# Experts of a mixture in column tiles: four experts at a time, 96 rows each, weights through a ring of seven slots

## What is computed

```python
N_GROUPS, EXPERTS_PER_GROUP, TOP_K, D_MODEL, D_FF_EXPERT = 4, 8, 2, 1024, 512   # 32 experts
pg = softmax(x @ wrg + brg);  g_val, g_idx = top_k(pg, 1)          # one group per token
le = (x @ wre + bre)[group g_idx];  e_val, e_idx = top_k(le, 2)    # two experts of that group
e_w = softmax(e_val) * g_val;  expert = g_idx * 8 + e_idx
for every token and each of its two experts e:
    y[token] += e_w * ((silu(x @ wg[e]) * (x @ wu[e])) @ wd[e])
return h + y
```

## Time and profile before

| | us |
|---|---|
| median of 3 runs | 2239.81 |
| lowest and highest | 2235.87, 2240.45 |
| span of the profiled execution | 2236.3 |
| PE busy | 1933.4 (86%) |
| DVE, ACT, POOL busy | 584.9, 479.2, 104.5 |
| PE in the three products of the experts | 229.1 + 225.0 + 225.1 |

### The profile page before, as it was taken

The page is one execution under the profiler, slowest core; times in us unless marked ns, Lnnn a source line. Parts: engine busy times, 40 slices in busy tenths (PEclk is TensorE's granted clock), DMA queues, the critical chain, the costliest instruction groups (busy, mean ns, idle before and its releaser), DMA issues. The chain is left out here.

```text
span 2236.3 us, 18672 instructions
## 1 busy us (share of the span) xinstructions
PE 1933.4 (86%) x6294; PEld 1013.3 (45%) x6294; DVE 584.9 (26%) x1144; ACT 479.2 (21%) x1059; POOL 104.5 (5%) x143
## 2 busy tenths in 40 slices
PE   7899896888875789899599999379999999999990
PEld 3354743555542345555344544244444444444440
DVE  2111203676651233223222222411111111111114
ACT  2162101333322333333200000001111111111110
POOL 0000001000030000000000000000000000000003
PEclk9999997999996899989699999679999999999995
DMA  3310004111137100100151221357888888888847
GB/s 124 118 35 28 30 18 171 44 46 38 38 113 235 59 38 24 47 23 24 64 220 72 103 113 47 135 225 293 356 318 349 324 338 334 326 348 319 355 193 263
DMA packets 87624, 354.84 MB, mean 159 GB/s; under 512 B 14424, under 2 KB 38016, under 8 KB 74000
## 3 DMA queue, kind: packets, MB, share of 16 engines
q1 hardware_dynamic: 65488, 282.86, 33.1%
q0 software_dynamic: 12032, 43.52, 5.6%
q10 hardware_dynamic: 10064, 27.94, 3.2%
HBM read 292.81 MB, written 54.41 MB: 155 GB/s over the span
## 5 line engine op out<-in xcount | busy, mean ns | idle before, releaser
L1968 PE MATMUL ps<-eg,xsT 128*128 128x512 f32 x512 | 229.1, 601 | 4.5 <-DVE hid L1930 3.2
L1995 PE MATMUL ps<-ed,hT 128*128 128x512 f32 x512 | 225.1, 592 | 1.8 <-ACT hT L1899 1.8
L1981 PE MATMUL ps<-eu,xsT 128*128 128x512 f32 x512 | 225.0, 592 | 0.0
L1271 PE MATMUL ps<-wg,xt 128*128 128x512 f32 x432 | 207.8, 637 | 13.3 <-DMA xt<-xn_dram 8.8
L1941 DVE TENSOR_TENSOR xsT<-ps,wnT 128x512 f32<-128x512 f32 x64 | 41.2, 686 | 590.8 <-PE ps L1955 590.8
L243 PE MATMUL ps<-wbuf,wide 128*128 128x512 f32 (+3 forms) x464 | 171.4, 529 | 9.3 <-issue 9.3
L1968 PEld LDWEIGHTS ps<-eg,xsT 128*128 128x128 f32 x512 | 98.6, 193 | 129.2 <-issue 127.4
L1995 PEld LDWEIGHTS ps<-ed,hT 128*128 128x128 f32 x512 | 94.9, 190 | 109.7 <-issue 107.6
L1981 PEld LDWEIGHTS ps<-eu,xsT 128*128 128x128 f32 x512 | 94.9, 190 | 107.6 <-issue 107.6
L1271 PEld LDWEIGHTS ps<-wg,xt 128*128 128x128 f32 x432 | 85.9, 205 | 125.9 <-issue 110.2
L238 PE MATMUL ps<-wide,wbuf 128*128 128x512 f32 (+1 forms) x384 | 131.0, 505 | 11.2 <-issue 11.2
(11 more groups left out here) (321 smaller groups left out, 1908.5 us busy)
## 6 DMA issues: line engine op xcount, KB each, us to landing
eg<-w_expert_gate SPq DMA_DIRECT2D x32, 2048.0 KB, 13.2
eu<-w_expert_up SPq DMA_DIRECT2D x32, 2048.0 KB, 17.7
ed<-w_expert_down SPq DMA_DIRECT2D x32, 2048.0 KB, 8.4
y_dram<-ys ACTq DMA_DIRECT2D x32, 512.0 KB, 10.7
gt<-g_dram SPq DMA_DIRECT2D x9, 1024.0 KB, 5.8
y_dram<-wide POOLq DMA_DIRECT2D x34, 256.0 KB, 4.1
wbuf<-w_in SPq DMA_DIRECT2D x8, 1024.0 KB, 5.5
g_dram<-gb SPq DMA_DIRECT2D x9, 768.0 KB, 3.3
```

Of the source, the lines that this page charges most:

```text
L1271: last = pe.matmul(ps[2][:, :], xt[:, k * P:(k + 1) * P], wg[:, j, k, :], start=(k == 0), stop=(k == KC - 1))
L1968: last = pe.matmul(ps[0][:, :], xsT[:, n, k * P:(k + 1) * P], wg[n][:, k, :], start=(k == 0), stop=(k == KC - 1))
L1981: last = pe.matmul(ps[1][:, :], xsT[:, n, k * P:(k + 1) * P], wu[n][:, k, :], start=(k == 0), stop=(k == KC - 1))
L1995: last = pe.matmul(ps[2 + c][:, :], hT[:, k * P:(k + 1) * P], wd[n1][:, k, c * 512:c * 512 + 512], start=(k == 0), stop=(k == FF // P - 1))
```

## The change

`experts` now takes four experts at a time, expert q of each of the four groups, so that there are eight rounds of q. A block of `T.slots` holds 32 rows of each of the four experts, member a at partitions 32a to 32a + 31, and three such blocks (`ROUNDS`) give each expert 96 rows. There are 24 main blocks and 23 overflow blocks. A product of 128x128 weights becomes four products of 128x32, one for each expert: the same contraction rows, 32 columns of the array each, and 32 partitions of the PSUM bank each. The weights move through a ring of seven slots of 2 MB, each with one slice of the weights of all four experts; a slot is reloaded when its products are done. The stage is written out without a loop. `route` computes the slots for this layout, with some more steps on DVE.

A load now waits for the slice seven loads earlier, whatever matrix that was, and a partition's 16 KB come from four places in memory. The diff, cut to its core:

```diff
-OVER = (2 * NT * P - 1) // P
-NBLK = NE + OVER
+SUB = 32
+ROUNDS = 3
+CAP = SUB * ROUNDS
+NMAIN = EPG * ROUNDS
+OVER = 2 * NT * P // (CAP + 1)
+NBLK = NMAIN + OVER
+LOADS = 12
+RING = 7
+def expert_load(eng, A, T, n):
+    q, m = divmod(n, LOADS)
+    if m < 8:
+        w = (A.w_expert_gate if m < 4 else A.w_expert_up)[0].rearrange("(g e) (p k) f -> p g e (k f)", e=EPG, k=KC)
+        src = w[:, :, q, m % 4 * D:m % 4 * D + D]
+    else:
+        w = A.w_expert_down[0].rearrange("(g e) (p k) d -> p g e (k d)", e=EPG, k=FF // P)
+        src = w[:, :, q, (m - 8) * D:(m - 7) * D]
+    eng.dma_start(T.ring[:, n % RING, :, :], src).then_inc(T.s_ring[n % RING], 16)
...
-            with pool.Fori(NE + NT, NBLK) as b:
+            with pool.Fori(NMAIN + NT, NBLK) as b:
                 clear(b)
...
-                clear(i + NE)
+                clear(i + NMAIN)
...
+            for n in range(RING):
+                expert_load(sp, A, T, n)
...
+        def consumed(eng, n):
+            q, k = divmod(n, LOADS)
+            if k == 3:
+                eng.wait_ge(s_g, ROUNDS * (q + 1))
+            elif k == 7:
+                eng.wait_ge(s_u, ROUNDS * (q + 1))
+            elif k == 11:
+                eng.wait_ge(s_d1, ROUNDS * (q + 1))
+            else:
+                eng.wait_ge(s_use, 9 * q + k - k // 4 + 1)
...
+            for n in range(RING, LOADS * EPG):
+                consumed(sp, n - RING)
+                expert_load(sp, A, T, n)
...
-                    pool.tensor_copy(idx[:, n:n + 1], T.slots[:, ds(e, 1)] if not isinstance(e, int) else T.slots[:, e:e + 1])
-                    pool.drain()
-                    pool.indirect_dma_start(out=xs[:, n, :], out_offset=None, in_=T.x_dram,
+                    pool.indirect_dma_start(out=xs[:, r, :], out_offset=None, in_=T.x_dram,
...
+                for r in range(ROUNDS):
+                    act.wait_ge(s_hp, ROUNDS * q + r + 1)
+                    act.copy(hT[:, r, :, :], psz[r % 2][:, :].rearrange("p (k n) -> p k n", n=P)).then_inc(s_hc, 1)
...
+            member = lambda a: slice(SUB * a, SUB * a + SUB)
+            def rows_in(q, r):
+                n = ROUNDS * q + r
+                pe.wait_ge(s_xs[r], 16 * (q + 1))
+                if n:
+                    pe.wait_ge(s_xc, n)
...
+            def into_hidden(q, i, bank, done):
+                n = LOADS * q + i
+                landed(pe, n)
+                for r in range(ROUNDS):
+                    for h in range(2):
+                        k = 2 * (i % 4) + h
+                        for a in range(NG):
+                            last = pe.matmul(bank[r][member(a), :], xsT[:, q % 2, r, k, member(a)],
+                                             ring[:, n % RING, a, h * FF:(h + 1) * FF],
+                                             start=(k == 0), stop=(k == KC - 1))
...
+                hidden_rows(q, 0)
+                hidden_rows(q, 1)
+                for k in range(FK):
+                    landed(pe, LOADS * q + 8 + k)
+                for r in range(ROUNDS):
+                    pe.wait_ge(s_hc, ROUNDS * q + r + 1)
+                    for k in range(FK):
+                        last = out_product(q, k, r, 0)
+                    last.then_inc(s_d0, 1)
+                    if r == 0:
+                        hidden_rows(q, 2)
+                for k in range(FK):
+                    for r in range(ROUNDS):
+                        last = out_product(q, k, r, 1)
+                        if k == FK - 1:
+                            last.then_inc(s_d1, 1)
+                    if k < FK - 1:
+                        last.then_inc(s_use, 1)
```

More of the change, by code:

```diff
@@ L1825, in experts @@
         s_hc = m.sem("e_hc")
-        s_d = m.sem("e_d")
-        s_y = m.sem("e_y")
-        s_ow = [m.sem(f"e_ow{n}") for n in range(2)]
-        block = ctx.enter_context(nc.Block())
[L1831 to L1842, removed]
+        s_d0 = m.sem("e_d0")
@@ L1844, in _, with landed @@
+        def landed(eng, n):
+            eng.wait_ge(T.s_ring[n % RING], 16 * (n // RING + 1))
         @block.sync
         def _(sp):
[L1846 to L1861, removed]
@@ L1877, in _ @@
-            schedule(pool, step)
+            for q in range(EPG):
+                for r in range(ROUNDS):
+                    b = ROUNDS * q + r
+                    if q:
+                        pool.wait_ge(s_xp, b - ROUNDS + 1)
+                    pool.indirect_dma_start(out=xs[:, r, :], out_offset=None, in_=T.x_dram,
+                                            in_offset=bass.IndirectOffsetOnAxis(ap=T.slots[:, b:b + 1].bitcast(U32), axis=0)
+                                            ).then_inc(s_xs[r], 16)
@@ L1881, in _ @@
             act.preload_act_table_set("natural_log_exp_and_others")
[L1883 to L1889, removed]
+            for q in range(EPG):
+                for r in range(ROUNDS):
+                    a = au[:, r, 0, :]
+                    act.wait_ge(s_g, ROUNDS * q + r + 1)
+                    if q:
+                        act.wait_ge(s_ow[r], 16 * q)
+                    act.activation(a, psx[r][:, :], ACT.Exp, scale=-1.0)
@@ L1908, in _ @@
-            schedule(act, step)
-            for n in range(2):
-                act.wait_ge(s_ow[n], 16 * NE // 2)
+                    act.activation(a, a, ACT.Exp, scale=-1.0).then_inc(s_sg, 1)
+                for r in range(ROUNDS):
+                    act.wait_ge(s_hp, ROUNDS * q + r + 1)
+                    act.copy(hT[:, r, :, :], psz[r % 2][:, :].rearrange("p (k n) -> p k n", n=P)).then_inc(s_hc, 1)
+                for r in range(ROUNDS):
+                    act.wait_ge(s_d0, ROUNDS * q + r + 1)
+                    act.copy(au[:, r, 0, :], psx[r][:, :]).then_inc(s_y0, 1)
@@ L1912, in _ @@
+                for r in range(ROUNDS):
+                    b = ROUNDS * q + r
+                    act.wait_ge(s_d1, b + 1)
+                    act.copy(au[:, r, 1, :], psy[r][:, :])
+                    act.drain().then_inc(s_y1, 1)
+                    act.dma_start(T.y_dram[b], au[:, r, :, :].rearrange("p c n -> p (c n)")).then_inc(s_ow[r], 16)
+            for r in range(ROUNDS):
+                act.wait_ge(s_ow[r], 16 * EPG)
         @block.vector
         def _(dve):
-            def rows(e):
-                dve.wait_ge(s_xp, e + 1)
@@ new lines, in hidden_rows, with out_product @@
+            def hidden_rows(q, r):
+                pe.wait_ge(s_h, ROUNDS * q + r + 1)
+                if r == 2:
+                    pe.wait_ge(s_hc, ROUNDS * q + 1)
+                for k in range(FK):
+                    last = pe.transpose(psz[r % 2][:, k * P:(k + 1) * P], au[:, r, 1, k * P:(k + 1) * P], T.eye[:, :])
+                last.then_inc(s_hp, 1)
+            def out_product(q, k, r, c):
+                n = LOADS * q + 8 + k
+                for a in range(NG):
+                    last = pe.matmul((psx, psy)[c][r][member(a), :], hT[:, r, k, member(a)],
+                                     ring[:, n % RING, a, c * 512:c * 512 + 512], start=(k == 0), stop=(k == FK - 1))
+                return last
@@ L2006, in overflow @@
         m = Memory(nc, ctx)
-        wg = m.sb("vg", [P, KC, FF])
-        wu = m.sb("vu", [P, KC, FF])
-        wd = m.sb("vd", [P, FF // P, D])
+        wg, wu = (T.ring[:, n, :, :].rearrange("p a (k f) -> p (a k) f", f=FF) for n in range(2))
+        wd = T.ring[:, 2, :, :]
         xs = m.sb("vxs", [P, D])
@@ L2224, in program @@
         m = Memory(nc, ctx)
[L2225 to L2227 removed]
+        T.ring = m.sb("ring", [P, RING, NG, D])
+        T.s_ring = [m.sem(f"e_ring{n}") for n in range(RING)]
         T.wts = m.sb("wts_", [P, 2, NT])
```

210 lines of the change are left out of this document (85 added, 125 removed).

## The result

| | before | after |
|---|---|---|
| median, us | 2237.84 (4 runs) | 2146.65 (4 runs, 2144.71 to 2148.96) |
| ratio | | 0.959, 95% interval 0.958 to 0.960 |
| span of the profiled execution, us | 2236.3 | 2147.3 |
| end of the last down product, us | 2182.7 | 2092.9 |

The change makes the kernel 91 us faster. The forecast was 139.5 us, so the sign and the mechanism held and a third of the gain is missing. The first view is the timeline of TensorE (PE) over one group of four experts, from its first gate product to the next group's (the columns are those of the earlier trace rows, with the idle time ahead of a piece and what ended it in brackets). Between the two timeline rows at 1707.93 and 1769.04 lie the whole gate and up products of the group, its transposes and the first part of its down products.

The account below looks back on a forecast made before the run. TensorE was taken to bound the expert stage before, the weights' loop after. The stage's -142.9 us and +3.4 for clears sum to -139.5 off the 2239.8 us median: about 2100 us, range 2064 to 2188.

Parts of the forecast that it names:

- Column tiles: Expert products: four 128x32 tiles run at once, so a step costs one product, 0.859 us, and 72 steps 61.8 us.
- rivals 1 to 3: Expert products: two tiles at a time, 2576 us (0.12); gain of three, 2244 us (0.09); no overlap, 3564 us (0.04).
- TensorE's group: TensorE's own work for four experts: 61.8 products + 3.96 transposes + 1.0 changes + 0.8 hidden copy = 67.6 us.
- A change between transposes and tiled products: TensorE in the expert stage: 0.1 us each, ten per group, 1.0 us per group; ends 0 and 0.3.
- the wait for the first hidden copy: Between hidden transposes and down products: ACT's copy plus the transposes' tail, about 0.8 us once per group.
- The weights' loop: Seven-slot ring: nine loads must land between first down-slot release and next down products; 70.3 us per group, over TensorE's 67.6.
- 46.0 + 7.7 + 3.0 + 13.6 = 70.3 us: Ring period: nine loads, gathers and output writes, issue to landing, then 15 steps, transposes and changes until the next release.
- the first three terms: Ring period: nine loads at 410 GB/s 46.0 us, gathers and output writes 7.7, issue to landing 3.0.
- forecast idle time of 3 us: Before the down products: TensorE waits some 3 us per group for the last down load.
- 66 to 82 us per group: Expert stage, later groups: 66 if changes are free and loads just keep up, 82 if DMA moves only 334 GB/s.
- Start: Expert stage's first product at 1480.7 us: route +2.2, three serial rounds of rows +6.7, less about 1 for POOL's index copy.
- Clears: Recurrence start: POOL clears 14 blocks, not 8; +3.4 us taken (0 to 7.8), TensorE's w_in wait from 16.17 to some 20.

## Why the prediction was right, and where it was not

**Column tiles: right.** The factor of four holds, 0.4294 against 0.108 us a record, and rivals 1 to 3 fell with the first row of the timeline. The extrapolation from tiles that differ in rows to tiles that share them held. The Trainium skill's rule of strict program order ("TensorE: Matmul & The Clock Gate", "Part 3: Packing small matmuls") does not agree with the starts of four tiles within 0.02 us; its 3.07 times for row tiles stands against 4.0 measured here for column tiles.

**TensorE's group: right at 67.57 against 67.6, by two errors that cancel.** A change between transposes and tiled products costs 0.14 us, not 0.1 (from 1733.80 to 1740.11 are 6.31 us, eight transposes of 0.88 and 12 passes of 5.15 in it, for two changes), 0.4 us more per group; the wait for the first hidden copy is 0.33 us, not 0.8.

**The weights' loop: the right mechanism, mis-sized; this is the step that failed.** "46.0 + 7.7 + 3.0 + 13.6 = 70.3 us" measured 78.3 in the group above. The queue of SP shows it (start, us from the first issue to the last, count):

```profile
1700.45 0.37 SPq L83 DMA_DIRECT2D ring<-w_expert_gate  x1
...
1740.24 38.88 SPq L83 DMA_DIRECT2D ring<-w_expert_gate  x4
```

From the load at 1700.45, the first into a freed down slot, to the down products at 1762.46 are 62.0 us, where the first three terms give 56.7; from there to the next such load, 1740.24 + 38.88 - 0.37 = 1778.75, are 16.3 us instead of 13.6.

- Of the first 5.3 us, 2.0 are the restart: 6 us at 271 GB/s instead of 410. The term took the full rate for a queue that is never idle, yet the loop itself makes it idle. About 1.2 us are issue and landing: by single packets 1.05 us from issue to the first and 3.2 from the last to the product, 4.25 against the 3.0 that was estimated from the shortest landing of a gate load. From 1712 to 1730 the engines moved 390 GB/s, 0.9 us. Some 1 us is not placed; part of it may be the slow restart again, which lasts to 1710 us, longer than the 6 us counted here.
- Of the 2.7 us, 2.4 are the clock after the wait, shown by the version that computes through it: there the same stretch, from 1764.12 to the next such load at 1777.99, takes 13.9 us. The prediction named a clock below 1.00 as a danger for the whole stage; it did not ask what its own forecast idle time of 3 us would do to it.

The seven later groups took 539.4 us (1553.52 to 2092.9) instead of 489.5: 49.9 of the 53 us that the stage's end is late. That the time still fell within the range is partly luck: its bounds of 66 to 82 us per group took in a DMA rate that is lower throughout, not the restart and the clock that made the difference.

**Start: 1484.41 instead of 1480.7.** Route +2.1 (from its first step to the slots 44.3 us before, 46.4 after), as summed at 2.2; slots to first product 16.0 instead of 9.5, +6.5 where 6.7 less 1 was summed; the other 3.0 us were there before route began, where the thirteen profiles differ by 9.9 us. The first group, 69.1 us with the clock's rise, is as summed.

**Clears: the wait was foreseen, its worth stays open.** "From 16.17 to some 20" measured 21.69. Whether the +3.4 us on the end are right is not shown: the runs moved clears to a place where they cost as much. The same operation of DVE in the ninth and last tile begins at 669.0 to 675.6 us in the nine profiles with fourteen clears at the start, 673.2 on the average, and at 669.4 in the one profile of the kernel before. That would fit 3.4, but one profile cannot tell it.

## What to carry to other kernels

Before costing a ring of buffers at the full DMA rate, go around it once: what frees the first slot, how many loads must land before the next such release, and whether the queue or the computing engine falls idle on the way, since each idle stretch then costs again in a slow restart and a low clock. An order of loops that takes the buffered slices one by one (wait for one, use it up, free it) was worth 63 to 70 us here without moving a byte less. And a wait that gets shorter early in the program counts only if the end of the stage comes sooner too: work that was moved to shorten it can cost the same where it now stands.

## What was not expected of the hardware

- A DMA queue that had run out of loads, or nearly so, restarted at 254 to 271 GB/s with its engines over 0.9 busy, in loads whose steady rate was 410 to 421; the packets of the first load after the pause took 233 ns on the average (228 in the version that computes through the wait), and 160 to 168 in most others. The cause is not shown.
- Eight microseconds without work took the granted clock from 1.00 to 0.50, and it was still at 0.50 from 1762.50 to 1766.00, while TensorE was busy again (0.90 over 1767 to 1769).
- Four column tiles on the same 128 rows ran in f32 at four times the pace (240 records in 25.93 us), also when four records of one tile stand in a row (26.00 us).
- One operation of DVE in the recurrence, the same 128x512 product, took 2.37 us with one clear of POOL behind a tile and 6.83 with two, and 0.69 in the other tiles. In both cases products of POOL ran beside it; that these hold it up is not shown.
